# A fused two-block kernel: 14 of 22 up-projection pairs a layer by seven products, with two weight sums formed by adding transfers

## What is computed

```python
h = rmsnorm(x, ffn_norm[l])
u = h @ ffn_w_up[l]                       # 1024 -> 2 * 2816
a, bv = u[..., :D_FF], u[..., D_FF:]
a = causal_dwconv(a, ffn_conv_w[l], ffn_conv_b[l])
x = x + (jax.nn.silu(a) * bv) @ ffn_w_down[l]
```

## Time and profile before

| | us |
|---|---|
| median of 3 runs (1962.96 to 1963.34) | 1962.99 |
| span of the profiled execution | 1959.6 |
| what lies around it, against the median | 3.4 |
| TensorE busy | 1937.3 |
| VectorE busy | 1276.2 |
| ScalarE busy | 875.9 |
| GpSimd busy | 30.0 |

### The profile page before, as it was taken

One profiled execution on the slowest core, in us unless ns is written; L12 is line 12 of the kernel. 1 busy time (PEld: TensorE's weight loads), 2 busy tenths in 40 slices (PEclk: granted clock), 3 DMA queues, 4 the chain that ended last, 5 costly groups with the idle time before them and its releaser, 6 DMA issues.

```text
span 1959.6 us, 30739 instructions
## 1 busy us (share of the span) xinstructions
PE 1937.3 (99%) x11610; PEld 1631.9 (83%) x11610; DVE 1276.2 (65%) x1564; ACT 875.9 (45%) x1281; POOL 30.0 (2%) x60
## 2 busy tenths in 40 slices
PE   7999999999999999999999999999999999999998
PEld 5887889898887897889898888997777777888888
DVE  6866788887656866788877646846664644534435
ACT  5345453444323345453344322344445666544343
POOL 2001000000000001000000000000000000000000
PEclk9999999999999999999999999999999999999999
DMA  7213133333324213133333223533332222232322
GB/s 197 87 39 105 44 108 101 92 107 102 102 76 126 74 49 108 44 108 89 104 98 111 94 84 97 173 82 98 85 112 67 61 82 65 87 118 76 100 88 82
DMA packets 241075, 182.38 MB, mean 93 GB/s; under 512 B 12970, under 2 KB 232360, under 8 KB 240574
## 3 DMA queue, kind: packets, MB, share of 16 engines
q1 hardware_dynamic: 238368, 177.37, 30.7%
q0 software_dynamic: 2160, 2.22, 0.6%
q10 hardware_dynamic: 430, 1.23, 0.2%
HBM read 168.21 MB, written 2.10 MB: 87 GB/s over the span
## 4 chain that ended last, share of the span: by engine, by line
PE 89%; DVE 6%; issue 2%; ACT 1%; DMA 1%; DVEq 0%; SPq 0%; POOL 0%; ACTq 0%
PE ps L881 19%; PE ps L883 19%; PE ps L882 19%; PE ps L1420 4%; PE ps L1419 4%; PE ps L1418 4%; PE ps L668 2%; PE ps L644 2%; PE ps L657 2%; DVE amat L2238 2%; PE ps L1318 1%; PE ps L1317 1%; PE ps L1316 1%; PE ps L520 1%; PE ps L489 1%
## 5 line engine op out<-in xcount | busy, mean ns | idle before, releaser
L881 PE MATMUL ps<-h_hi,w_hi 128*128 128x512 f32 (+1 forms) x1232 | 477.1, 387 | 1.1 <-ACT qk L1623 0.7
L883 PE MATMUL ps<-h_hi,w_lo 128*128 128x512 f32 (+1 forms) x1232 | 468.0, 380 | 0.0
L882 PE MATMUL ps<-h_lo,w_hi 128*128 128x512 f32 (+1 forms) x1232 | 465.6, 378 | 0.0
L2124 DVE TENSOR_TENSOR w_lo<-w_raw,w_hi 128x2048 fp32r<-128x2048 f32 (+3 forms) x110 | 227.0, 2063 | 147.1 <-ACT w_hi L1630 142.1
L881 PEld LDWEIGHTS ps<-h_hi,w_hi 128*128 128x128 f32 x1232 | 231.6, 188 | 51.1 <-issue 8.0
L883 PEld LDWEIGHTS ps<-h_hi,w_lo 128*128 128x128 f32 x1232 | 231.4, 188 | 44.4
L882 PEld LDWEIGHTS ps<-h_lo,w_hi 128*128 128x128 f32 x1232 | 231.6, 188 | 43.8 <-issue 1.9
L1630 ACT ACTIVATE w_hi<-w_raw 128x2048 fp32r<-128x2048 f32 (+3 forms) x108 | 186.7, 1729 | 180.2 <-PE ps L1420 124.9
L2632 DVE TENSOR_TENSOR w_lo<-w_raw,w_hi 128x1024 fp32r<-128x1024 f32 (+1 forms) x118 | 126.5, 1113 | 155.6 <-ACT w_hi L1951 154.8
L881 PE MATMUL ps<-w_hi,h_hi 128*128 128x256 f32 x544 | 152.4, 280 | 0.3 <-DVE h_lo L855 0.3
L882 PE MATMUL ps<-w_lo,h_hi 128*128 128x256 f32 x544 | 150.7, 277 | 0.0
(11 more groups left out here) (437 smaller groups left out, 3469.8 us busy)
## 6 DMA issues: line engine op xcount, KB each, us to landing
w_raw<-in_ffn_w_up_dram SPq DMA_DIRECT2D x88, 512.0 KB, 4.5
w_raw<-in_w_in_dram SPq DMA_DIRECT2D x41, 1024.0 KB, 5.3
w_raw<-in_w_in_dram SPq DMA_DIRECT2D x32, 512.0 KB, 5.2
w_raw<-in_ffn_w_down_dram SPq DMA_DIRECT2D x32, 512.0 KB, 4.3
w_raw<-in_w_out_dram SPq DMA_DIRECT2D x12, 1024.0 KB, 5.2
w_raw<-in_ffn_w_down_dram SPq DMA_DIRECT2D x16, 384.0 KB, 3.6
swapped<-qk SPq DMA_DIRECT2D x96, 64.0 KB, 2.0
w_raw<-in_w_mem_kv_dram SPq DMA_DIRECT2D x4, 1024.0 KB, 5.1
```

The source lines that it names most:

```text
L881: pe.matmul(dst, lh, rh, start=first and j == 0, stop=False)
L882: pe.matmul(dst, lh, rl, start=False, stop=False)
L883: ins = pe.matmul(dst, ll, rh, start=False, stop=last and j == len(order) - 1)
L2124: dve.tensor_tensor(w_lo[:, slot, 0:n], w_raw[:, slot, 0:n], w_hi[:, slot, 0:n].bitcast(F32), ALU.subtract).then_inc(sem("w_split"), 1)
```

## The change

Fourteen pairs of 22 are fast, even ones too; `PLAIN_F` names the plain ones. The loops over pairs are written out. For a fast pair f, slot s = f % 2:

- TensorE: four of the seven products go, one after the other, into one PSUM area that is read between them (`chain`, bank 5 + 2s), two into one half of the value bank (2s + 1), the seventh by itself into its other half. The sums that VectorE made afterwards so arise in the accumulation. `skip_group_check` lets a group be read while it is open. After each product, TensorE goes on to one in the other bank, and waits (`kept`) for ScalarE's copy of the area before it adds to it again.
- ScalarE: four copies of 128 x 256 a fast pair (`keep`), two into `hid`, one into another bank, one into `c_sum`.
- VectorE: `first_gate` (256 columns), `gate_fast` (512), `value_fast` (512), and the product with silu. Two of the four weight sums are left.
- SyncE loads for a fast pair a third piece, 256 KB of the same weights, into `s_first[s]`.
- GpSimd, once all three have landed, issues two transfers that add 256 KB of weights each, one onto a block of `w_raw[slot]` in place, one onto `s_first[s]`. ScalarE's split of that chunk and VectorE's two sums wait for both.
- Three semaphores of the program's start are merged into two, and some buffers have other places.

```diff
-FAST_FROM, FAST_TO = 3, 19
+PLAIN_F = (0, 1, 2, 7, 12, 17, 20, 21)
+FAST_F = tuple(f for f in range(KF) if f not in PLAIN_F)
...
+                for f in range(KF):
+                    s = f % 2
+                    sp.wait_ge(sem("w_split"), upto(sp, "w_split", C_UP + f - 1))
+                    for half in range(2):
+                        sp.dma_start(slot_view(w_raw, s, KD)[:, :, half * P:half * P + P],
+                                     wsrc("ffn_w_up", l, f * P + half * FF, P)).then_inc(sem(f"w_loaded{s}"), 16)
+                    if f in FAST_NO:
+                        if f - 2 in FAST_NO or f - 4 in FAST_NO:
+                            sp.wait_ge(sem("s_split"), upto(sp, "s_split", 2 * FAST_NO[f - 2 if f - 2 in FAST_NO else f - 4] + 1))
+                        sp.dma_start(s_first[s], wsrc("ffn_w_up", l, f * P, P, 0, 4)).then_inc(sem(f"w_loaded{s}"), 16)
...
+                for f in FAST_F:
+                    s = f % 2
+                    up = lambda k0, c0: A["ffn_w_up"][l:l + 1, k0 * P:(k0 + 4) * P, c0:c0 + P].rearrange("a (k p) n -> p (a k) n", p=P)
+                    pool.wait_ge(sem(f"w_loaded{s}"), upto(pool, f"w_loaded{s}", up_loaded(f)))
+                    pool.dma_start(slot_view(w_raw, s, KD)[:, 0:4, 0:P], up(0, FF + f * P), accum_op=ALU.add).then_inc(
+                        sem(f"sums_landed{s}"), 16)
+                    pool.dma_start(s_first[s], up(4, f * P), accum_op=ALU.add).then_inc(sem(f"sums_landed{s}"), 16)
...
+                    product(pe, chain, block(0, 1), tokens_(0, 0), range(4), last=False, read_open=True).then_inc(sem("part_done"), 1)
...
+                    pe.wait_ge(sem("s_split"), upto(pe, "s_split", 2 * n + 1))
+                    product(pe, part(value, 0), summed(0), mixed_t(0), range(4), last=False, read_open=True).then_inc(sem("part_done"), 1)
+                    kept(1)
+                    pe.wait_ge(sem("s_split"), upto(pe, "s_split", 2 * n + 2))
+                    product(pe, chain, summed(1), mixed_t(1), range(4), first=False, last=False, read_open=True).then_inc(sem("part_done"), 1)
+                    kept(2)
+                    product(pe, part(value, 0), summed(2), tokens_(4, 1), range(4), first=False, read_open=True).then_inc(sem("part_done"), 1)
+                    kept(3)
+                    product(pe, chain, block(0, 0), mixed_t(2), range(4), first=False, last=False, read_open=True).then_inc(sem("part_done"), 1)
+                    product(pe, part(value, 1), block(4, 1), tokens_(4, 0), range(4), read_open=True).then_inc(sem("tile_done"), 1)
+                    kept(4)
+                    product(pe, chain, block(4, 0), mixed_t(3), range(4), first=False, read_open=True).then_inc(sem("tile_done"), 1)
...
+                    if f in FAST_NO:
+                        chain = part(5 + 2 * s, 1)
+                        next_up_high(f)
+                        if f == 19:
+                            act.wait_ge(sem("s_split"), upto(act, "s_split", 2 * FAST_NO[f] + 1))
+                        keep(f, 1, 1, hid[:, f, 256:512], chain)
+                        keep(f, 2, 2, part(4 + 2 * s, 0), part(2 * s + 1, 0))
+                        conv_start(f - 1, (f - 1) % 2)
+                        keep(f, 3, 3, hid[:, f, 0:256], chain)
+                        if f + 1 in FAST_NO:
+                            sums_high(f + 1, 0, 1)
+                            sums_high(f + 1, 1, 3)
+                        if FAST_NO[f]:
+                            act.wait_ge(sem("fast_sum"), upto(act, "fast_sum", 2 * FAST_NO[f] - 1))
+                        keep(f, 4, 5, c_sum[:], chain)
+                        conv_silu(f - 1)
...
+                for f in range(3, KF + 1):
+                    if f - 1 in FAST_NO:
+                        gate_fast(f - 1)
+                        value_fast(f - 1)
+                    else:
+                        gate_tile(f - 1, (f - 1) % 2)
+                    if f < KF:
+                        split_low(C_UP + f + 1, (f + 1) % 2, KD)
+                    if f in FAST_NO:
+                        conv_taps(f - 1, (f - 1) % 2)
+                    if f + 1 in FAST_NO:
+                        sums_low(f + 1, 0, 1)
+                        sums_low(f + 1, 1, 3)
+                    if f + 2 in FAST_NO:
+                        weight_sums(f + 2)
+                    if f in FAST_NO:
+                        first_gate(f)
+                    else:
+                        conv_taps(f - 1, (f - 1) % 2)
+                    if f - 1 in FAST_NO:
+                        hidden_fast(f - 1)
+                    else:
+                        hidden(f - 1, plain((f - 1) % 2))
```

More of the change, by code:

```diff
@@ L321, in layer_chunks @@
             return out
-        n_dma = [2, 2, 2] + [1] * 6 + [4, 2, 2] + [2] * 4 + [1] * 4 + [2] * (KF + CH_DOWN)
+        up_loaded = lambda f: 16 * sum(n_dma[f % 2::2][:(C_UP + f) // 2 + 1])
+        sums_landed = lambda f: 32 * sum(1 for u in FAST_F if u <= f and u % 2 == f % 2)
+        n_dma = [2, 2, 2] + [1] * 6 + [4, 2, 2] + [2] * 4 + [1] * 4 + [3 if f in FAST_NO else 2 for f in range(KF)] + [2] * CH_DOWN
         def two(name, c0, n=256, k0=0, k=None):
@@ L872, in normed, with product @@
             return full
-        def product(pe, dst, lhs, rhs, order, first=True, last=True, ready=None):
+        def product(pe, dst, lhs, rhs, order, first=True, last=True, ready=None, read_open=False):
             for j, k in enumerate(order):
@@ L880, in product @@
                     pe.wait_ge(sem("h_lo"), upto(pe, "h_lo", ready + j + 1))
-                pe.matmul(dst, lh, rh, start=first and j == 0, stop=False)
-                pe.matmul(dst, lh, rl, start=False, stop=False)
-                ins = pe.matmul(dst, ll, rh, start=False, stop=last and j == len(order) - 1)
+                pe.matmul(dst, lh, rh, start=first and j == 0, stop=False, skip_group_check=read_open)
+                pe.matmul(dst, lh, rl, start=False, stop=False, skip_group_check=read_open)
+                ins = pe.matmul(dst, ll, rh, start=False, stop=last and j == len(order) - 1, skip_group_check=read_open)
             return ins
@@ L1377, in fast_pair, with kept @@
                     part = lambda bank, c: ps[:, bank, c * 256:c * 256 + 256]
+                    chain, value = part(5 + 2 * s, 1), 2 * s + 1
+                    def kept(k):
+                        pe.wait_ge(sem("part_kept"), upto(pe, "part_kept", 4 * n + k))
                     split_ready(C_UP + f)
-                    pe.wait_ge(sem("tile_copied"), upto(pe, "tile_copied", t - 2))
-                    product(pe, part(5, 0), block(0, 1), tokens_(0, 0), range(4)).then_inc(sem("p1_done"), 1)
@@ L1388, in fast_pair @@
-                    product(pe, part(2, 0), summed(2), tokens_(4, 1), range(4)).then_inc(sem("tile_done"), 1)
-                up_tile(0, 0, 0)
-                sum_stat(pe, 8)
-                up_tile(0, 0, 1)
-                for f in range(1, FAST_FROM - 1):
-                    for half in range(2):
-                        up_tile(f // 2, f % 2, half)
-                with pe.Fori(0, FAST) as n:
-                    i = n + FAST_FROM // 2
-                    for half in range(2):
-                        up_tile(i, 0, half)
-                    fast_pair(i, n)
@@ L1892, in _ @@
[L1892 to L1901 removed]
+                sums_high(3, 0, 1)
+                sums_high(3, 1, 3)
@@ L2464, in conv_taps, with value_fast @@
+                def value_fast(f):
+                    s = f % 2
+                    dve.wait_ge(sem("part_kept"), upto(dve, "part_kept", 4 * FAST_NO[f] + 3))
+                    dve.wait_ge(sem("tile_done"), upto(dve, "tile_done", T_UP + 2 * f + 1))
+                    dve.tensor_tensor(hid[:, f, :], hid[:, f, :], ps[:, 2 * s + 1, :], ALU.add).then_inc(sem("fast_sum"), 1)
                 def conv_taps(f, slot):
@@ L2545, in _ @@
                 block_low(1)
[L2546 to L2547 removed]
+                weight_sums(3)
                 gate_tile(1, 1)
@@ L2573, in _ @@
[L2573 to L2583 removed]
+                sums_low(3, 0, 1)
```

254 lines of the change are left out of this document (115 added, 139 removed).

## The result

The changed kernel takes 2010.29 us (median of 4 runs, 2007.34 to 2012.53), the kernel before 1963.15 beside it: ratio 1.024, 95% interval 1.0228 to 1.0252. It is slower by 47 us, where 10 us less was forecast, and it lies outside the range.

What follows compares the result with a forecast made beforehand. TensorE's streaming, 99% busy, was taken as the bound. Ten pairs at 1.02 us gave -10.2, all else hidden: span 1959.6 to 1949.4, plus 3.4 around it, 1952.8 us; range 1951.5 to 1967.

Steps and rivals of the forecast that it cites:

- The gross gain: Up-projection on TensorE: ten more fast pairs over two layers, each 1.02 us shorter than a plain one, 10.2 us saved.
- ScalarE and the open groups: ScalarE's round in a fast pair: all four copies are done before TensorE wants them, load 7.6 of 9.97 us, cost nothing.
- rival 1: TensorE waits for ScalarE's first copy in each of 28 fast pairs: 5.6 us back, 1958.4; chance 0.17.
- (a): ScalarE's first work in a fast pair, the split of the next weights: 1.91 us, to 2.18 after the pair's start.
- (b): ScalarE's first copy in a fast pair: 0.39 us, to 2.5, wanted by TensorE at 2.6, margin 0.1 us.
- VectorE: VectorE's round in a fast pair: durations sum to 9.6 us, margin 0.1 to 0.2 us a pair, cost nothing.
- Rival 2: VectorE becomes the bound in groups of four, its adds waiting for GpSimd issues: 7 us back, 1960; chance 0.13.
- rival 4: The down stage starts 1 us late in each of two layers, its margin down to 0.4: 1955; chance 0.06.
- Transfers: Third load and GpSimd's two adding transfers per fast pair: sums landed 6 us after GpSimd's wake, 7.5 free, so hidden.
- D: Time from GpSimd's wake to the second adding transfer's landing: taken as 6 us, bounds 3.8 to 12.1, 7.5 free.
- rival 3: Adding transfers are late at s_first and w_raw's first block: at 11 us to landing, 24 us lost, 1977; chance 0.16.
- 3.1 us late before TensorE pays: Groups of four fast pairs: VectorE may be 3.1 us late, by ScalarE's third copy, before TensorE waits.

Runs made afterwards that it cites:

- no_adds: Changed kernel without its 56 adding transfers, their waits made waits for the three loads (three of four weight sums wrong): 1947.98 us, ratio 0.9918.
- dve_sums_9: Changed kernel with no adding transfers or third load, VectorE forming all four sums, at the nine fast pairs of before: 1959.76 us, ratio 0.9985.
- plain_copies: Changed kernel with its GpSimd transfers overwriting instead of adding, same sizes and rows (three of four sums wrong): 1946.90 us, ratio 0.992.
- dve_sums_13: Changed kernel with no adding transfers or third load, VectorE forming all four sums, 13 fast pairs in groups of at most three: 1964.88 us, ratio 1.0002.
- dve_sums_14: Changed kernel with no adding transfers or third load, VectorE forming all four sums, 14 fast pairs kept: 1965.67 us, ratio 1.0016.
- half_adding: Changed kernel with each adding transfer cut to two of its four blocks (half of two sums left out): 1952.88 us, a single run.

## Why the prediction was wrong, step by step

**The gross gain** was sized too small. no_adds, where no sum comes late, has 16.1 us less than before by its ratio (0.0082 x 1963.4), not 10.2: 1948, below my 1951.5. Fast pairs run in 9.76 us from the second group on (timeline of no_adds, four pairs in 39.04):

```profile
388.86 0.28 PE L885 MATMUL ps<-h_hi,w_hi 128*128 128x256 f32 x1
...
398.62 0.28 PE L885 MATMUL ps<-h_hi,w_hi 128*128 128x256 f32 x1
...
427.90 0.39 PE L885 MATMUL ps<-h_hi,w_hi 128*128 128x512 f32 x1
```

With 9.76 the sum is ten new fast pairs at 11.00 - 9.76 and 18 old ones at 9.98 - 9.76, 16.4 us, less 0.5 for the slower first groups (39.31 in place of 39.04). Twelve matmuls with weight tiles take 1.36 us there and 1.41 in most fast pairs of the kernel before. The pace was to be seen before, once in each layer, had I read more fast pairs (timeline of the kernel before, the one of layer 2 in 9.76):

```profile
920.87 0.28 PE L881 MATMUL ps<-h_hi,w_hi 128*128 128x256 f32 x1
...
930.63 0.39 PE L881 MATMUL ps<-h_hi,w_hi 128*128 128x512 f32 x1
```

Its other fast pairs take 9.96 to 10.05. dve_sums_9 has the pace with the fast pairs of before and no transfers of the change, so it comes with the new structure (order of products, PSUM areas, copies, written-out loops); what in it sets the pace stays open. One term was named wrongly, at no cost to the sum: of the 3.4 us that I put down to start and end around the span, most runs with both a time and a span show 1.8, some up to 2.9 (2009.77 and 2008.0 here).

**ScalarE and the open groups**: right. In no_adds TensorE has no wait at all in 280 to 490 us, so the margin of 0.1 us at copy 1 held, and rival 1 did not occur by itself: in ten fast pairs of layer 1, copy 1 ended 2.4 to 2.5 us after the pair's start. Two sums were loose: (a) and (b) end at 2.57 and not 2.5, and ScalarE's terms add up to 6.6 us a pair and not 7.6; measured are 6.1. **VectorE**: right as to its work, 8.8 to 9.0 us in a full fast pair of the first group. **Rival 2** fell. Of VectorE's weight splits in the kernel after, 21 ran while an adding transfer was being issued and 20 in the same stages did not, and both kinds take 2290 ns on average; its sums take 692 ns, as before. The rule of the Trainium skill (SBUF — State Buffer, Who interferes with whom), by which a VectorE instruction with two SBUF inputs and a GpSimd one that reads SBUF hold each other up, has no price here: the issue of an adding transfer did not hold VectorE up. **The down stage** (rival 4) was in time: no wait of TensorE at its start in no_adds (480.38).

**Transfers: this step failed**, in D = 6 us and "then it hides", and as rival 3 put it, at both the places it named. The issues cost 1.27 and 1.8 us, not 1.0 each. The first transfer lands 4.6 us (median) after its issue, the second 6.1 into s_raw and 7.9 into s_first. Where VectorE waited in layer 1, D was 7.1 to 10.8 for the 7.5 that were free. My lower bound of 3.8 belongs nearer to copies (4.3 to 5.8 measured), and "nearest to the plain rows" was the wrong side to lean to; the bounds themselves held. What 6 left out went, for the larger part, with the loads beside: with none in flight or due within 3.1 us D was 6.3 to 6.7 (once 7.7), and the long ones are those with SyncE's next loads in flight. That is read from the traces and not shown by a run of its own. The working had no term for adding transfers and loads that meet. The loads pay for it too: pair 6's three loads, beside two adding transfers, took 10.4 us from issue to the last landing, against 8.2 in plain_copies (293.83 to 302.02) on the same pair.

**Rival 3 had the mechanism and the side, and its price was less than half.** For D = 11 it gave 24 us lost; 63 were lost (against plain_copies) at a median D of 8.9, which by its own working would have cost nothing. Two things were missed. First, the "3.1 us late before TensorE pays": I took it from one round of fast pairs, and at a group's edges less is free. VectorE's sums of pair 5 stand ahead of the product with silu of plain pair 2, whose bank TensorE wants 1.4 us into pair 4; with sums at t0 + 8.26, product done at t0 + 10.9 and wanted at t0 + 11.3, 0.4 us was free there, not 3.1. In a plain round the sums stand ahead of the taps, so silu, ScalarE's next split and copy 1 wait with them. That is the second long wait; its timeline in the kernel after:

```profile
350.71 0.69 DVE L2547 TENSOR_TENSOR s_raw<-s_first,w_raw 128x512 f32<-128x512 f32 x1 [3.47 <-DMA s_first<-in_ffn_w_up_dram]
...
353.61 0.63 ACT L1866 ACTIVATE rms_a<-rms_a 128x512 f32<-128x512 f32 x1 [9.84 <-DVE rms_a L2521]
354.42 1.91 ACT L1654 ACTIVATE w_hi<-w_raw 128x2048 fp32r<-128x2048 f32 x1 [0.18 <-ACT rms_a L1866]
...
356.24 0.36 ACT L1893 ACTIVATE hid<-ps 128x256 f32<-128x256 f32 x1
...
356.73 0.58 PE L885 MATMUL ps<-t_hi,s_hi 128*128 128x256 f32 x1 [4.26 <-ACT hid L1893]
```

Second, the clock: a stall was priced at its length, and each long one cost some 2 us more. Putting the product ahead of the sums in VectorE's order was not tried.

**The chances**: 0.16 for rival 3 was too low. D was the one cost without any row, and its bounds (3.8 to 12.1) reached past the 10.2 that decided even by my own low price.

## What to carry to other kernels

An operation that no row prices is first run by itself, and beside the traffic that it will meet, or its middle isn't leaned to the cheap side. Adding in a transfer made 256 KB cost 528 packets for 80 and over twice the time of the DMA engines, while the plain copy of the same bytes was hidden. Before a wait is put into an in-order queue, list for every round, those at the edges of a pattern too, what stands behind it and who wants that first. And one adding transfer, with the rest of the sums rewritten over its result, kept VectorE's round short enough for 14 to 16 fast pairs, at about half of D.

## What was not expected of the hardware

- The granted clock fell to 1.2 GHz inside TensorE's idle times of 4.3 to 7.2 us, and it was low for 2.8 to 5.1 us of the work that followed. Behind idle times of 2.4 us (dve_sums_13 and dve_sums_14) it fell too, for 3.4 us. Idle pieces of 1.6 us and less in the up-projection were not followed by a fall, and neither was one of 2.5 us in half_adding (at 446.01). The Trainium skill (TensorE: Matmul & The Clock Gate, What's actually happening) has an idle TensorE go back to 1.2 GHz; the trace agrees (0.50 from 306.00 on).
- A 128x256 matmul's pace has two values at the same granted clock of 1.00: 0.113 us (12 in 1.36) and 0.118 (12 in 1.41), for weight tiles only; products with s tiles stay at 1.44.
- Halving the rows of an adding transfer left GpSimd's issue at 1.19 of 1.27 us, so that issue hardly goes by rows.
- In the window 304.00:305.00 the DMA engines' mean busy share reads 1.27. It passes 1 without adding transfers too (1.16 in 300:301 of the kernel before), so the records of transfers overlap, and the share can't be read as capacity used or left.
